# Fourier columns first in the projection, transforms between its blocks, output weights split meanwhile

## The reference

```python
h = rmsnorm(x, norm_mix)
u = h @ w_in                                   # 1024 x 2048
u_b, u_c, u_x, u_f = split(u, 4)               # 512 columns each
v = u_c * u_x
y_conv = rmsnorm(u_b * (conv of v over 3 neighbouring rows, conv_w), g_conv)
y_four = rmsnorm(real(fft2 of u_f over rows and over 64 columns), g_fourier)
x = x + concat(y_conv, y_four) @ w_out
# then: rmsnorm, router, softmax over 16 experts, each expert takes its top 2*rows/16 rows,
# SwiGLU of width 2816 on them, weighted sum back into x, final rmsnorm
```

## Time and profile before

| | us |
|---|---|
| median of 3 runs (2579.91 to 2581.01) | 2580.14 |
| the profiled execution | 2579.22 |
| its span, first to last instruction | 2577.3 |
| TensorE busy in the span | 2438.6 (95%) |
| VectorE busy | 1650.2 (64%) |
| ScalarE busy | 1344.1 (52%) |
| GpSimd busy | 194.7 (8%) |

### The profile page before, as it was taken

How to read it: one execution, slowest core, us unless ns; L and a number is a source line. 1 busy time by engine, 2 the same in 40 slices (tenths; PEclk the granted TensorE clock), 3 DMA queues, 4 the chain that set the end, 5 groups by cost and what they waited for, 6 DMA issues and landing times.

```text
span 2577.3 us, 45156 instructions
## 1 busy us (share of the span) xinstructions
PE 2438.6 (95%) x18269; PEld 1915.0 (74%) x18269; DVE 1650.2 (64%) x1350; ACT 1344.1 (52%) x1233; POOL 194.7 (8%) x191
## 2 busy tenths in 40 slices
PE   5999879759999999999999999999999999999994
PEld 4888768647777777777777777777777777777773
DVE  4344455967676767667676666676767676666674
ACT  5222322325555556556555555565656565556563
POOL 0010120010101010101010101001010101010000
PEclk8999889879999999999999999999999999999997
DMA  3110242426878786868787878787877878787866
GB/s 119 41 33 25 99 168 107 173 98 258 317 264 316 269 299 262 298 261 299 279 305 280 307 280 307 279 309 269 313 275 285 301 264 322 266 320 267 318 261 222
DMA packets 296891, 627.28 MB, mean 243 GB/s; under 512 B 21392, under 2 KB 72848, under 8 KB 296464
## 3 DMA queue, kind: packets, MB, share of 16 engines
q1 hardware_dynamic: 288336, 598.88, 63.1%
q0 software_dynamic: 8384, 25.71, 3.7%
HBM read 598.31 MB, written 26.21 MB: 242 GB/s over the span
## 4 chain that ended last, share of the span: by engine, by line
PE 90%; DVE 5%; DMA 2%; ACT 1%; issue 1%; SPq 0%; POOL 0%; DVEq 0%; ACTq 0%; POOLq 0%
PE ps L353 20%; PE ps L354 19%; PE ps L355 19%; PE ps L1336 12%; PE ps L1150 9%; PE ps L1344 6%; PE ps L1354 1%; DVE i L935 1%; DVE v L933 1%; DVE A L937 1%; DMA raw<-in_w_gate_dram 1%; PE ps L1295 1%; DMA wo_raw<-in_w_out_dram 1%; DVE wof_l L873 0%; PE ps L1363 0%
## 5 line engine op out<-in xcount | busy, mean ns | idle before, releaser
L1060 DVE TENSOR_TENSOR spl_l<-raw,spl_h 128x2048 fp32r<-128x2048 f32 x528 | 1209.3, 2292 | 553.5 <-ACT spl_h L704 548.4
L704 ACT ACTIVATE spl_h<-raw 128x2048 fp32r<-128x2048 f32 x528 | 1012.1, 1917 | 576.5 <-PE ps L355 447.3
L353 PE MATMUL ps<-spl_h,xT 128*128 128x512 f32 x1408 | 555.0, 394 | 3.2 <-DVE xT L1065 2.5
L354 PE MATMUL ps<-spl_l,xT 128*128 128x512 f32 x1408 | 549.8, 390 | 0.0
L355 PE MATMUL ps<-spl_h,xT 128*128 128x512 f32 x1408 | 548.8, 390 | 0.0
L353 PEld LDWEIGHTS ps<-spl_h,xT 128*128 128x128 f32 x1408 | 264.7, 188 | 78.8 <-issue 22.3
L1336 PE MATMUL ps<-raw,xTs 128*32 128x256 f32 (+1 forms) x6144 | 314.2, 362 | 0.0
L355 PEld LDWEIGHTS ps<-spl_h,xT 128*128 128x128 f32 x1408 | 264.8, 188 | 56.1
L354 PEld LDWEIGHTS ps<-spl_l,xT 128*128 128x128 f32 x1408 | 264.8, 188 | 53.3
L353 PE MATMUL ps<-spl_h,g 128*128 128x512 f32 x704 | 278.0, 395 | 0.0
L354 PE MATMUL ps<-spl_l,g 128*128 128x512 f32 x704 | 274.4, 390 | 0.0
(11 more groups left out here) (199 smaller groups left out, 1961.5 us busy)
## 6 DMA issues: line engine op xcount, KB each, us to landing
raw<-in_w_up_dram SPq DMA_DIRECT2D x352, 512.0 KB, 8.3
raw<-in_w_gate_dram SPq DMA_DIRECT2D x352, 512.0 KB, 9.6
raw<-in_w_down_dram SPq DMA_DIRECT2D x176, 1024.0 KB, 14.9
win_raw<-in_w_in_dram SPq DMA_DIRECT2D x16, 512.0 KB, 3.8
xt<-in_x_dram SPq DMA_DIRECT2D x10, 512.0 KB, 8.3
xr<-in_x_dram SPq DMA_DIRECT2D x10, 512.0 KB, 4.0
acc_dram<-xr SPq DMA_DIRECT2D x10, 512.0 KB, 2.6
xn_dram<-xn SPq DMA_DIRECT2D x10, 512.0 KB, 2.9
```

The source lines that it names most:

```text
L353: eng.matmul(o, a_h, b_h, start=first, stop=False, skip_group_check=True)
L354: eng.matmul(o, a_h, b_l, start=False, stop=False, skip_group_check=True)
L704: act.activation(spl_h[:, i % SPL, :], raw[:, slot_of(i), :], ACT.Copy).then_inc(sh_ok, 1)
L1060: dve.tensor_tensor(spl_l[:, i % SPL, :], raw[:, slot_of(i), :], spl_h[:, i % SPL, :].bitcast(F32), ALU.subtract).then_inc(sl_ok, 1)
```

## The change

- The projection begins with the four Fourier blocks. The first two of them go in three parts each (rows 0 to 511, 512 to 1023, 1024 to 1279), with the transposes of tiles 4 to 9 between the k steps of the first parts. The first part waits for four tiles. The x tiles are turned in banks 4 to 7.
- The Fourier transforms of column block j are cut into pieces which stand between the k steps of later blocks: `channels(j, p)`, five pieces of two tiles, in block j + 2 at k = 3 to 7; `waves(j, i)`, three pieces, in block j + 3 at k = 0 to 2. They use banks 6 and 7. Y_h, Y_l hold one column block, AB_h and AB_l two.
- The tables are loaded once seven tiles are scaled. GpSimd's sums of the Fourier half follow the last transform, and their norm sums stand in block 10. The convolution's squares are made by ScalarE, GpSimd only adds; its norm sums stand in the first row tile.
- w_out is loaded in whole 128 x 1024 pieces into buffers of their own: four for the convolution half after block 12's weights, split in block 14's step; four for the Fourier half from the middle of block 15, split at the start of the rows.
- EARLY is 3, and the early units wait for the second norm sums. The unit in slot 4 (unit 7) and all behind it wait for `routed`, since small routing tiles lie in slots 4 and 5.
- The loops over the projection are written out. Many buffers lie elsewhere.

The diff at its core (`sums_of`, `gated`, `taps`, `conv_out`, `conv_copy`, `first_tap`, `channels_hi`, `sines` hold the instructions of before for one block):

```diff
-EARLY = 4
+EARLY = 3
+PROJ = 4 * JH
+PIECES = TILES // 2
...
+            def load_win(n):
+                if n < JH:
+                    col = 3 * DH + n * P
+                else:
+                    j, q = divmod(n - JH, 3)
+                    col = (1, 2, 0)[q] * DH + j * P
+                sp.dma_start(win_raw[:, n % 2, :, :], win_v[:, :, col:col + P]).then_inc(win_in[n % 2], 16)
...
+            sp.dma_start(gmix[:, :], norm_mix[0].rearrange("(k p) -> p k", p=P), allow_slow_non_contiguous=True).then_inc(gmix_in, 16)
+            sp.dma_start(xt[:, 0, :], x_t[0]).then_inc(x_in[0], 16)
+            load_win(0)
+            for t in range(1, 5):
+                sp.dma_start(xt[:, t, :], x_t[t]).then_inc(x_in[t], 16)
+            load_win(1)
+            for t in range(5, TILES):
+                sp.dma_start(xt[:, t, :], x_t[t]).then_inc(x_in[t], 16)
...
-            with nc.Fori(0, 2, engines=(sp.engine,), hint_back_edge=True) as jj:
-                for q in range(6):
-                    sp.wait_ge(winl_ok, jj * 6 + q + 1)
-                    sp.sem_inc(lone, 1)
-                    sp.dma_start(win_raw[:, q % 2, :, :],
-                                 win_v2[jj, :, :, (1, 2, 0)[q % 3], q // 3, :]).then_inc(win_in[q % 2], 16)
...
-            for n in range(2 * KD):
-                if n < 2:
-                    sp.wait_ge(dd_done, TILES)
-                else:
-                    sp.wait_ge(wol_ok, n - 1)
-                sp.dma_start(wo_raw[:, n % 2, :], wout_v[n // 2][:, (n % 2) * DH:(n % 2 + 1) * DH]).then_inc(wo_in[n % 2], 16)
+            for n in range(2, PROJ):
+                sp.wait_ge(winl_ok, n - 1)
+                load_win(n)
+                if n == 12:
+                    sp.wait_ge(nrm_ps, 1)
+                    for k in range(JH):
+                        sp.dma_start(woc_raw[:, k, :], wout_v[k]).then_inc(woc_in, 16)
+            sp.wait_ge(hT_half, 1)
+            for k in range(JH):
+                sp.dma_start(wof_raw[:, k, :], wout_v[JH + k]).then_inc(wof_in[k // 2], 16)
...
-            sp.wait_ge(ds_done, 3 * JH)
+            sp.wait_ge(u_done, PROJ)
...
+            sp.wait_ge(nrm_ps, 2)
             for i in range(EARLY):
                 load_unit(0, i)
...
+                if slot_of(i) == 4:
+                    sp.wait_ge(routed, 1)
                 if i >= RAW:
...
-            pool.wait_ge(u_done, 2 + 16)
...
             sv_ = dft_s.rearrange("h p n -> p h n")
+            pool.wait_ge(xs_ok, 7)
             pool.dma_start(tab_h[:, :, :].rearrange("p b n -> p (b n)"), sv_[:, 0, 0:HB * LARGE]).then_inc(tab_in, 16)
             pool.dma_start(tab_l[:, :, :].rearrange("p b n -> p (b n)"), sv_[:, 1, 0:HB * LARGE]).then_inc(tab_in, 16)
-            pool.wait_ge(dd_done, TILES)
             pool.dma_start(tsm[:, :, :], sv_[:, :, HB * LARGE:]).then_inc(tab_in, 16)
...
+                pool.wait_ge(sqc_ok, j + 1)
+                if j > 1:
+                    pool.wait_ge(qs_ok, j - 1)
+                pool.tensor_tensor(qc[:, :], qc[:, :], sqc[:, :], ALU.add).then_inc(qs_ok, 1)
...
+            def win_hi(n):
+                act.wait_ge(win_in[n % 2], 16 * (n // 2 + 1))
+                if n == 0:
+                    act.wait_ge(gmix_in, 16)
+                if n >= 2:
+                    act.wait_ge(u_done, n - 1)
+                for k in range(KD):
+                    last = act.activation(win_h[:, n % 2, k, :], win_raw[:, n % 2, k, :], ACT.Copy, scale=gmix[:, k:k + 1])
+                last.then_inc(winh_ok, 1)
...
             square_x(1)
+            win_hi(0)
             for t in range(TILES):
                 if t + 2 < TILES:
                     square_x(t + 2)
                 act.wait_ge(xT_ps, t + 1)
...
+            def halves(j):
+                u = bank(3 * (j % 2), 3)
+                act.wait_ge(u_done, j + 1)
+                if j:
+                    act.wait_ge(ab_ok, 4 * j)
+                act.activation(tmp[:, 0:SEQ // 2], u[:, SEQ // 2:SEQ], ACT.Copy).then_inc(tmp_ok, 1)
+                act.activation(tmp[:, SEQ // 2:T // 2], u[:, SEQ + DEC // 2:T], ACT.Copy).then_inc(tmp_ok, 1)
...
+            def sums_hi(j):
+                act.wait_ge(ab_ok, 4 * (j + 1))
+                if j >= 2:
+                    act.wait_ge(dd_done, PIECES * (j - 1))
+                act.activation(AB_h[j % 2][:, :], sums[:, :], ACT.Copy).then_inc(abh_ok, 1)
...
+            for n in range(1, PROJ):
+                if n <= JH:
+                    halves(n - 1)
+                j, q = divmod(n - 1 - JH, 3)
+                if n > JH and q == 0:
+                    conv_copy(j)
+                if n + 1 < PROJ:
+                    win_hi(n + 1)
+                if n <= JH:
+                    sums_hi(n - 1)
+                if n > JH and q == 1:
+                    first_tap(j)
+                if n > JH and q == 2:
+                    conv_square(j)
+                if 3 <= n < 3 + JH:
+                    sines(n - 3)
+                if 2 <= n < 2 + JH:
+                    channels_hi(n - 2)
+                if n == 11:
+                    act.wait_ge(nrm_ps, 1)
+                    act.activation(rm[:, 1, :], bank(7)[:, 16:16 + TILES], ACT.Sqrt, bias=eps[:, 0:1], scale=1.0 / DH).then_inc(rn_rt, 1)
+                if n == 14:
+                    for k in range(JH):
+                        wo_hi(k)
             def stage_hi(t, s):
                 act.wait_ge(of_done, t + 1)
-                if isinstance(t, int) and t == 0:
...
             stage_hi(0, 0)
+            wo_hi(JH)
+            wo_hi(JH + 1)
+            conv_square(JH - 1)
+            wo_hi(JH + 2)
+            wo_hi(JH + 3)
             act.wait_ge(nrm_ps, 2)
...
+                if n > JH and q == 1:
+                    gated(j)
+                if n > JH and q == 2:
+                    conv_out(j)
...
+                    for k in range(JH):
+                        wo_lo(k)
+            conv_out(JH - 1)
...
+            def project(n, t0, t1, between=None):
...
-                last.then_inc(u_done, 1)
-            pe.wait_ge(hTl_ok, TILES)
-            with nc.Fori(0, 2, engines=(pe.engine,), hint_back_edge=True) as jj:
-                for q in range(6):
-                    n, j = jj * 6 + q, jj * 2 + q // 3
...
+            def channels(j, p):
+                if p == 0:
+                    pe.wait_ge(abl_ok, j + 1)
+                    if j:
+                        pe.wait_ge(yf_ok, 8 * j)
                     else:
-                        pe.wait_ge(uc_ok, j + 1)
...
+            def waves(j, i):
+                if i == 0:
+                    pe.wait_ge(Yl_ok, PIECES * (j + 1))
+                    if j == 0:
+                        pe.wait_ge(tab_in, 48)
+                else:
+                    pe.wait_ge(yf_ok, 8 * j + 2 * i)
...
+            project(0, 0, 512, more_x({1: 4, 4: 5}))
+            pe.wait_ge(winl_ok, 2)
+            project(1, 0, 512, more_x({1: 6, 4: 7, 7: 8}))
+            pe.wait_ge(hTl_ok, 8)
+            project(0, 512, 1024, more_x({2: 9}))
+            pe.wait_ge(hTl_ok, 9)
+            project(1, 512, 1024)
+            pe.wait_ge(hTl_ok, TILES)
+            project(0, 1024, T)
+            project(1, 1024, T)
...
+            def posts(n):
+                def after(k):
+                    if 3 <= n < 3 + JH and k < 3:
+                        waves(n - 3, k)
+                    if 2 <= n < 2 + JH and k >= 3:
+                        channels(n - 2, k - 3)
+                    if n == 10 and k == 3:
+                        pe.wait_ge(qf_ok, 1)
+                        norm_sums(qf, 16)
+                return after
+            for n in range(2, PROJ):
+                pe.wait_ge(winl_ok, n + 1)
+                if n - 2 < JH:
+                    pe.wait_ge(ab_ok, 4 * (n - 1))
+                else:
+                    j, q = divmod(n - 2 - JH, 3)
+                    pe.wait_ge((uc_ok, v_ok, y_ok)[q], j + 1)
+                project(n, 0, T, posts(n))
...
                 if not before:
-                    pe.wait_ge(yf_ok, 8 * JH)
-                    pe.wait_ge(qf_ok, 1)
-                    norm_sums(qf, 16)
+                    pe.wait_ge(qs_ok, JH - 1)
+                    pe.wait_ge(rn_rt, 1)
+                    norm_sums(qc, 0)
+                    pe.wait_ge(wol_ok, KD)
...
+            pe.wait_ge(wol_ok, JH)
+            pe.wait_ge(y_ok, JH)
             rows(0, 0, False)
```

More of the change, by code:

```diff
@@ L255, in build @@
         qfs_ok = sem("qfs_ok")
-        wo_in = [sem(f"wo_in{s}") for s in range(2)]
+        hT_half = sem("hT_half")
+        woc_in = sem("woc_in")
+        wof_in = [sem(f"wof_in{k}") for k in range(2)]
         woh_ok = sem("woh_ok")
@@ L1132, in _, with turn_x @@
         def _(pe):
-            pe.wait_ge(ident_ok, 4)
-            for t in range(TILES):
+            def turn_x(t):
                 pe.wait_ge(xs_ok, t + 1)
@@ L1167, in _ @@
-            for j in range(JH):
-                pe.wait_ge(winl_ok, 12 + j + 3)
```

(64 more changed lines are left out.)

403 lines of the change are left out of this document (185 added, 218 removed).

## The result

| us | before | after |
|---|---|---|
| median | 2580.57 (4 runs) | 2604.94 (4 runs, 2602.51 to 2606.96) |
| the profiled execution | 2579.22 | 2605.27 |
| its span | 2577.3 | 2603.4 |

What follows compares the result with a forecast made beforehand. TensorE was taken as the bound, thin only from 0 to 43.4 and 270.8 to 351.5 us. A gain of 36.6 less 3.0 for the fetch gave -33.6 from 2579.2, plus 0.9 to the median: 2546 us, range 2535 to 2561.

Steps and rivals of the forecast that it cites:

- nothing that the diff does there is on TensorE: From 533.4 us to the end: moves only by beginning earlier or by its first transfers; TensorE busy 1994 of 2044 us.
- the expert stretch as long as before: Sign of a right forecast: the experts' part keeps its length, while the first expert starts 34 us earlier.
- Projection begins: Head: four x tiles are whole at 26.2 us and the projection starts there instead of at 43.44.
- Block 2: Head: third projection block starts at 64.9 us instead of 73.3, after waiting 2.7 for its weights; the head gives 8.4.
- Sum of waits 4.8: Projection: TensorE waits for transform pieces to be emptied in blocks 3 to 6, 4.8 us in all; bounds 0 and 38.
- Block 8's low split beside GpSimd: Block 7: VectorE's weight split ends with GpSimd's squares near 13.5 us, TensorE arrives at 14.1; hidden, otherwise 1 to 3 us.
- the clock rival: Lower clock holds for half of the head's 33.6 us of work, costing 17 us: 2563 us; chance 0.11.
- 3.7 us from there to the first output product: After the projection's end at 311.8: last convolution product, high copies and low half, so first output product at 315.5, against 351.57.
- 12.4 from there to the second half: First row: last weight splits delay norm sums and second half to 324.2 us, before at 360.82.
- Gain at this point: At the first row's norm sums and second half: 36.6 us earlier than before, passing unchanged through rows and routing.
- The fetch beside the burst: After routing: the first expert's row fetch shares transfer engines with units 7 to 10, costing 3 us; bounds 0 and 5.7.
- The slower rival: Projection: 32 transform pieces each wait for a 2.44 us run of weight splits, 78 us in all: 2619 us; chance 0.04.

Runs made afterwards that it cites:

- slot 136: The kernel after with only the head of TensorE's expert loop placed at instruction slot 136 of a 256-slot fetch block: 2553.72 us, ratio 0.990.
- 231: The kernel after itself, its loop head's slot read off the trace, not set: 2604.94 us, ratio 1.0095.
- slot 239: The kernel after with the expert loop's head placed 17 instructions ahead of its fetch block's end: 2623.56 us, ratio 1.0172.
- slot 0: Expert loop's head placed at a fetch block's first slot: in the kernel after 2637.43 us, ratio 1.0225; in the kernel before 2663.51 us, ratio 1.0323.
- slot 220: The kernel before with the expert loop's head placed 36 instructions ahead of its fetch block's end: 2604.63 us, ratio 1.0099.
- the runs in which the burst came later: The kernel after, head at slot 136, units 7 to 10 held until first gathered rows land: 2549.94 us; with sums ahead of weight splits: 2555.42, in blocks 3-5 only: 2546.21.
- Slot 190: The kernel after with the expert loop's head placed 66 slots ahead of its fetch block's end: 2562.88 us (2 runs), ratio 0.9933.

## Why the prediction was wrong, by its steps

**The step that failed** is in the first paragraph: "nothing that the diff does there is on TensorE, so that part moves only if it begins earlier, or if its first transfers change", and at the end "the expert stretch as long as before". The stretch got 51 us longer without a change to any of TensorE's instructions in it: the new prologue moved their place in the fetch blocks, and TensorE stood idle for 34.9 us at its jumps and ran at the lower clock after them. Set back to slot 136, the same kernel loses nothing there. None of the rivals had it. The trace of before could not show it as a wait, since there was none: its loop lay well by luck. But it held 157 transfers of instructions and a loop that jumps back; a rival "the moved loop stalls at its jumps" stood open, with a price that only another kernel could give.

The Trainium skill, "Runtime: NRT & Kernel Launch", section "Instruction fetch mechanics", says that instructions are read ahead in blocks of 16 KiB and that a taken branch breaks this and can stall. The runs agree, and add the measure: 0, 1.3, 2.4, 3.3 or 4.5 us of idle time at a jump (slots 136, 220, 231, 239 and 0), by the place alone. The same section says that crossing a block's end is mostly hidden; behind a jump it was not with 17, 25 and 36 slots before it, and was with 66 and 120.

The other steps, prediction against the kernel after:

- Projection begins: 26.2, was 26.31. Block 2: 64.9, was 65.12, after 2.5 us of wait for the weights' low half. Right, and for the reason given.
- "Sum of waits 4.8", the second pieces of blocks 3 to 6: four waits, all on the wave sums, 6.7 us: 1.6, 1.6, 0.7 and 2.8 us, for 1.3, 1.3, 0.2 and 2.0. The mechanism right, the size 1.9 short.
- Block 8's low split beside GpSimd, "hidden, with half a microsecond to spare": it took 9.6 us and nothing waited for it. Right.
- The clock: in the start it was low as counted (0.50 from 26.3 to 31.1). Against the clock rival the prediction argued that the clock should hold through the 2.7 us ahead of block 2. It did not: it was granted 0.51 from 65.2 to 68.7, behind that wait, and again from 239.3 to 242.7, behind block 10's norm sums. The first 36 products behind the wait took 8.84 us in the kernel after and 7.29 in the one with slot 136, whose instructions are the same up to there, so this term differs from one run to the next. Together with the waits the projection ended 5.7 us late: 317.5, not 311.8. The rival came in small part: at half the pace these stretches cost some 4 us beyond the 1.7 counted (an estimate from their lengths), where it had 17.
- 3.7 us from there to the first output product: was 3.9. 12.4 from there to the second half: 330.8 - 317.5 = 13.3. Gain at this point 30.1 instead of 36.6: mis-sized. The waits and the way to the output lie inside their bounds; the lower clock behind the two waits had no term.
- The fetch beside the burst: +3.0 taken, +2.9 by the waits (13.8 against 10.9), and the runs in which the burst came later took back what they should. The first fetch landed 7.2 us after its issue, as forecast (6 to 8); before, that one took 4.5, not the 4.3 of the prediction, which is the second's. After, the fetch and the first turn that waits for it:

```profile
508.72 1.03 POOL L521 DMA_INDIRECT xg<-xn_dram,gidx  x1 [0.91 <-POOL gidx L518]
...
516.63 1.94 PE L1375 MATMUL ps<-ident,xg 128*128 128x128 f32 x8 [13.76 <-DMA xgs<-xn_dram,gidx]
```

- With the loop's place as before, the sum is 2553.7 against 2546 forecast, inside the range 2535 to 2561: 6.5 us from the projection and its end, the rest within what runs differ by.
- The slower rival (pieces behind whole runs of splits) did not come: the slower time has another cause.

## What to carry to other kernels

A loop that jumps back has one more property than its instructions: where its first one lies in the fetch block. Any edit ahead of it moves that, and the effect can exceed the edit's own. If TensorE's waits show "issue" once per iteration, set the head's slot, leave some 50 slots or more behind it in its block (at this loop's pace; an estimate from the table above), keep off the block's very start, and judge an edit only against kernels with the same slot. And before a piece of VectorE's work is moved behind one that releases GpSimd, price it at the pace it has beside GpSimd.

## What was not expected of the hardware

- A head at a block's very start is the worst place found: 4.5 us a jump in both kernels, though 256 slots lie behind it. There the stall stands at the jump itself: TensorE's branch record takes 5.4 us instead of 0.35, a block is asked for 2.8 to 3.0 us after the branch begins, and the branch ends some 2.5 us after that, as long as a block takes to come into use behind the other jumps (asked for at 3.4, run at 5.9). So it looks like the same wait with no slots left to cover it. Why the head's own block has to be fetched there was not tried and stays open: with this loop of 2059 instructions its end then lies about 11 slots into a block, and that or the head's slot may be the cause. The stalls by slots left are shown for heads at 220, 231 and 239, and none at 190 and 136.
- With TensorE otherwise fully busy, the lower clock followed none of 13 stalls with 1.3 us of idle time (slot 220), 7 of 13 with 2.4 us (the kernel after), 12 of 13 with 3.3 us (slot 239) and all 13 with 4.5 us (slot 0), each time for 3 to 7 us.
- Slot 190 without any stall was some 9 us slower than slot 136. Its two runs lie 10 us apart, so the size is uncertain; the cause is open.
- VectorE's split of weights beside GpSimd's sums took 17.2 us for 2.2, more than the 6.53 known: it began 1.6 us after GpSimd's 18 us of work and ended 0.4 us behind it.
